# Scan of a bidirectional RWKV-7 block: the next unit's six operand loads are issued by ScalarE at the end of its slot instead of by SyncE

## What is computed

```
state = state * w_t + (state @ -kk_t) (kk_t * a_t)^T + v_t k_t^T      # 64 x 64 per head
y_t   = state @ r_t
```

## Time and profile before

| | us |
|---|---|
| median of 3 runs | 3510.02 (3507.2 to 3510.7) |
| the profiled execution | 3510.56 |
| its span, first to last instruction | 3508.8 |
| TensorE busy | 3421.2 (98%) |
| GpSimd busy | 1681.6 (48%) |
| VectorE busy | 1507.3 (43%) |
| ScalarE busy | 1109.3 (32%) |

### The profile page before, as it was taken

One profiled execution on the slowest core, in us unless ns is written; L12 is line 12 of the kernel. 1 busy time (PEld: TensorE's weight loads), 2 busy tenths in 40 slices (PEclk: granted clock), 3 DMA queues, 4 the chain that ended last, 5 costly groups with the idle time before them and its releaser, 6 DMA issues.

```text
span 3508.8 us, 42655 instructions
## 1 busy us (share of the span) xinstructions
PE 3421.2 (98%) x16463; PEld 2785.3 (79%) x16463; DVE 1507.3 (43%) x1844; ACT 1109.3 (32%) x1756; POOL 1681.6 (48%) x1413
## 2 busy tenths in 40 slices
PE   7999999999998999999799999999999999999999
PEld 6777777777777988888578888888888888888887
DVE  3555445555667877874342023321331133213320
ACT  4333324444234554544342232211221122212221
POOL 4333333333338888887275434444443444444443
PEclk9999999999999999999899999999999999999999
DMA  4444444333355555553543323323333233333323
GB/s 153 120 126 126 123 120 150 115 111 91 105 146 122 127 130 143 123 135 92 201 144 120 120 84 96 96 91 102 96 96 102 90 96 97 99 102 96 96 90 114
DMA packets 663161, 402.25 MB, mean 115 GB/s; under 512 B 191374, under 2 KB 595018, under 8 KB 662506
## 3 DMA queue, kind: packets, MB, share of 16 engines
q1 hardware_dynamic: 663018, 400.34, 39.6%
HBM read 345.73 MB, written 54.53 MB: 114 GB/s over the span
## 4 chain that ended last, share of the span: by engine, by line
PE 50%; DVE 1%; ACT 0%; DMA 0%; POOL 0%; issue 0%; SPq 0%; DVEq 0%; ACTq 0%; POOLq 0%
PE f_bank L149 9%; PE f_bank L151 9%; PE f_bank L150 9%; PE f_bank L1952 5%; PE f_bank L1951 5%; PE f_bank L1953 5%; PE f_bank L1910 2%; PE f_bank L1912 2%; PE f_bank L1911 2%; PE f_bank L1855 1%; PE f_bank L1856 1%; PE f_bank L1857 1%; DMA act_plain<-yt 0%; PE f_bank L1888 0%; POOL w_lo_b L140 0%; PE f_bank L1864 0%
## 5 line engine op out<-in xcount | busy, mean ns | idle before, releaser
L140 POOL TENSOR_TENSOR w_lo_b<-w_raw_b,w_hi_b 128x2048 fp32r<-128x2048 f32 (+1 forms) x152 | 682.0, 4487 | 929.3 <-ACT w_hi_b L133 929.3
L1249 POOL TENSOR_TENSOR ring_w_rounded<-ring_w_plain,ring_w_hi 128x1024 fp32r<-128x1024 f32 x138 | 332.3, 2408 | 617.9 <-ACT ring_w_hi L1262 617.9
L149 PE MATMUL f_bank<-act_rounded,w_lo_b 128*128 128x512 f32 x1408 | 549.1, 390 | 2.4 <-POOL w_lo_b L140 1.2
L133 ACT CAST w_hi_b<-w_raw_b 128x2048 fp32r<-128x2048 f32 (+1 forms) x152 | 283.1, 1862 | 838.3 <-PE f_bank L1953 376.1
L151 PE MATMUL f_bank<-act_rounded,w_hi_b 128*128 128x512 f32 x1408 | 547.8, 389 | 0.0
L150 PE MATMUL f_bank<-act_rounded,w_hi_b 128*128 128x512 f32 x1408 | 547.8, 389 | 0.0
L1519 PE MATMUL slab_ps<-h_hi,ring_w_rounded 128*128 128x512 f32 x1088 | 450.2, 414 | 2.8 <-DVE h_lo L1374 2.5
L1520 PE MATMUL slab_ps<-h_lo,ring_w_hi 128*128 128x512 f32 x1088 | 425.3, 391 | 0.0
L1521 PE MATMUL slab_ps<-h_hi,ring_w_hi 128*128 128x512 f32 x1088 | 425.2, 391 | 0.0
L149 PEld LDWEIGHTS f_bank<-act_rounded,w_lo_b 128*128 128x128 f32 x1408 | 264.3, 188 | 57.5 <-issue 2.2
L151 PEld LDWEIGHTS f_bank<-act_rounded,w_hi_b 128*128 128x128 f32 x1408 | 264.3, 188 | 54.9
(11 more groups left out here) (342 smaller groups left out, 5593.5 us busy)
## 6 DMA issues: line engine op xcount, KB each, us to landing
ring_w_plain<-in_w_in_dram SPq DMA_DIRECT2D x190, 512.0 KB, 4.1
w_raw_b<-in_w_ffn_gate_dram SPq DMA_DIRECT2D x44, 1024.0 KB, 5.2
w_raw_b<-in_w_ffn_up_dram SPq DMA_DIRECT2D x44, 1024.0 KB, 5.2
w_raw_b<-in_w_ffn_down_dram SPq DMA_DIRECT2D x32, 1024.0 KB, 5.0
zt<-slab_out SPq DMA_DIRECT2D x65, 256.0 KB, 4.4
w_raw_b<-in_w_out_dram SPq DMA_DIRECT2D x16, 1024.0 KB, 5.0
w_raw_b<-in_w_ffn_down_dram SPq DMA_DIRECT2D x16, 768.0 KB, 4.4
zt<-lout SPq DMA_DIRECT2D x40, 256.0 KB, 4.6
```

The lines of the kernel that those rows point to most:

```text
L133: act.copy(g.w_hi[n.slot][:, 0:k, :], g.w_raw[n.slot][:, 0:k, :]).then_inc(g.w_hi_ready, 1)
L140: pool.tensor_tensor(g.w_lo[n.slot][:, 0:k, :], g.w_raw[n.slot][:, 0:k, :], g.w_hi[n.slot][:, 0:k, :].bitcast(F32), ALU.subtract).then_inc ...
L149: pe.matmul(bank, wl, hi[:, ka, :], start=start and j == 0, stop=False)
L1249: pool.tensor_tensor(raw_half(w_lo, h), raw_half(w_raw, h), hi_half(h).bitcast(F32), ALU.subtract).then_inc(lo_ready, 1)
```

## The change

The function `load` moves out of SyncE's program, takes the issuing engine as an argument, and is called by ScalarE at the end of each of its slots, behind the copy of half a gate slab. The two waits move with it. The very first load, `load(0)`, stays with SyncE.

```
+        def load(eng, n):
+            s, h, at = place(n)
+            rows = lambda base: zt[base + h * (NQ * P):base + (h + 1) * (NQ * P), at:at + CH].rearrange("(q p) c -> p q c", p=P)
+            for dst, base in ((sw_in, ROW_SW + s * RW), (kk_in, ROW_KK), (ic_in, ROW_IC + s * RW), (k_in, ROW_RKV + RW),
+                              (r_in, ROW_RKV), (v_in, ROW_RKV + 2 * RW)):
+                eng.dma_start(dst[:, :, :], rows(base)).then_inc(landed, 16)
...
             @block.sync
             def _(sp):
-                def load(n):
...
-                load(0)
+                load(sp, 0)
...
                     for h in next_halves(slot + 1)[1:]:
                         weights(h)
-                    if 0 <= w < NUNIT - 1:
-                        sp.wait_ge(taken_dve, DVE_AT["operands", w])
-                        sp.wait_ge(taken_act, ACT_AT["vbd", w])
-                        load(w + 1)
                     if 0 <= u < NUNIT:
...
                     for h in next_halves(slot + 1)[:1]:
                         high(h)
+                    w = unit_at(slot, "w")
+                    if 0 <= w < NUNIT - 1:
+                        act.wait_ge(taken_dve, DVE_AT["operands", w])
+                        act.wait_ge(taken_act, ACT_AT["vbd", w])
+                        load(act, w + 1)
```

## The result

The changed kernel takes 3527.32 us, the median of 5 runs (3522.24 to 3535.42), beside 3510.56 for the kernel before on the same chip. One of the five runs of the kernel before took 5190.07 us, and the ratio goes by the others. It is 1.0046, with a 95% interval of 1.0031 to 1.0061. The forecast was 3504.0, the range 3499 to 3520: wrong in sign, and outside the range. The profiled execution has 3527.32 us as well, 16.8 more than the one of before.

What follows compares the result with a forecast made beforehand. TensorE and GpSimd were taken to bound the scan side by side. At most 7.2 us gained, less 1.6 where TensorE is slower again, plus 0.5 at the start, gave 6.1: profiled 3504.5, median 3504.0, range 3499 to 3520.

Steps and rivals of the forecast that it cites:

- What it adds: ScalarE's six issues delay x1's copy and lx: 0.43 us lost into an odd slot, about 0.1 into an even one.
- The second term mis-sized: Length of the six-load group on ScalarE at SyncE's price, 0.507 us the usual issue: 3.12 us usually, 3.55 on average.
- the 0.5 us: Ahead of GpSimd's iteration 0: the `nb` store lands sooner without 512 KB before it, 0.5 us gained once (0 to 1.5).
- What was removed: In odd slots the loads go out earlier, 7.4 us in slot 21, so TensorE's 11.7 us of waits at yh go.
- 38.3 us a pair: TensorE's pair of slots without 14.6 us of waits: 38.3 us instead of 39.4, less than GpSimd's 38.65.
- The cap of 7.2 us: Gain bounded by GpSimd's idle time, 8.0 us in 7 waits, less 0.12 us for each handover that stays.
- GpSimd: GpSimd's chain in the scan: 38.65 us an iteration, assumed not to depend on what runs beside it.
- The check values: Signs of being right: small waits at `cum`, L811 and GpSimd, issues of 3.1 to 3.6 us, x1 of unit 30 earlier.
- The sign named for a wrong prediction: TensorE waits before lx (L768) for ScalarE's x1 more than 8 us, which was next to nothing before.
- rival 1: Two issuers obstruct each other in odd slots, groups up to 6.2 us: 10 us slower, 3520; chance 0.11.
- (2): An issue costs ScalarE more than SyncE, 0.8 us each, group 4.8: 16 us slower, 3526; chance 0.07.
- (3): Waits at yh go and as much appears before lx through the delayed x1: 3510, within 2; chance 0.15.

Runs made afterwards that it cites:

- hold of six copies: The kernel before, no DMA moved, but ScalarE waits for the operands and makes six unused chained copies, 2.6 us: 3507.65 us, ratio 0.9995.
- kernel 3: The changed kernel, but ScalarE issues the six loads only at the end of odd slots, SyncE in even ones: 3517.30 us, ratio 1.0012.
- hold of nine copies: The kernel before, no DMA moved, but ScalarE waits for the operands and makes nine unused chained copies, 3.9 us: 3521.04 us, ratio 1.0043.
- 5: The changed kernel, but SyncE sends the first half slab behind the `nb` store, not at the slot's start: 3512.38 us, ratio 1.0008.
- kernel 9: The changed kernel, but SyncE waits for ScalarE's copy of x1 before it issues the half slab: 3514.71 us, ratio 1.0007.
- 3.0 (hold): The kernel before, no DMA moved, but ScalarE waits for the operands and makes seven unused chained copies, 3.0 us: 3514.43 us, ratio 1.0000.
- kernel 11: The changed kernel, but ScalarE issues in even slots only and the first half slab goes behind the `nb` store: 3507.71 us, ratio 0.9989.
- kernel 7: The kernel before, all loads on SyncE, but the half slab goes out ahead of the six loads: 3510.50 us, ratio 1.0003.

## Why the prediction was wrong, point by point

**The step that failed** is the overlap claimed in this sentence of "What it adds": "*Into an even slot* `a_bd` is earlier: lx starts 4.3 to 6.8 us behind it", and the loss of "about 0.1" an even slot that came from it. The trace gives 23.5 us of waits at lx into the 13 even slots 2 to 26, 1.8 each. Into the 14 odd slots it gives 6.0 us, 0.43 each, which is what was forecast; the last 1.2 us stand at units 28, 29 and 31 and were there before.

Three things make up the 23.5 us. As an estimate, take the distances from `a_bd` to lx of the kernel before and put the group and the copies behind `a_bd`. With groups of 3.55 us the 13 slots lose about 4 us, 0.3 each, because a gate copy stands ahead of x1's in five of them and not in slot 18 alone. With the groups as measured, 4.28 us on average here, they lose about 10. The other 13 us can come only from cover that has shrunk: x1's weight loads began 2.2 us behind `a_bd` on average over these slots, and begin 1.0 behind it now (slot 7: 2.9 and 0.4). The prediction took this distance for fixed.

Why it shrank is not shown. One reading is that the cover was made of TensorE's own stalls, which the change was to remove: at yh TensorE was kept back, so x1 came late. For it: the distance stays at 2.2 with the hold of six copies, where the waits at yh stay. Against it: in kernel 3 these waits are gone and the distance is still 2.0. The other is that VectorE's operands come later because lx does (below). In the hold of nine copies, where only ScalarE's lateness was added, it is 1.55.

**The second term mis-sized** is the group: 3.55 us by the earlier trace rows, 3.92 measured. The price of one issue was right within 5%. What was left out is what the freed SyncE sends next: the prediction saw that the half slab moves away from the `nb` store, counted 0.5 us for it at the start of the chain, and didn't ask what it moves next to. The `nb` store did land sooner (SyncE's waits for it fall from 51.7 to 29.8 us), but iteration 0 starts at 1030.23, before 1030.03, so the 0.5 us didn't come. Kernels 5 and 9 show that this half is worth most of the loss: with the slab elsewhere the group is 3.4 or 3.3 us and the ratio 1.0008 or 1.0007. Ordered by how long ScalarE is kept behind the operands, all kernels that keep it at this place tell the same:

| ScalarE kept, us | waits at lx, us | ratio |
|---|---|---|
| 2.6 (hold) | 3.0 | 0.9995 |
| 3.0 (hold) | 7.7 | 1.0000 |
| 3.28 (9) | 10.0 | 1.0007 |
| 3.39 (5) | 13.8 | 1.0008 |
| 3.9 (hold) | 23.8 | 1.0043 |
| 3.92 (changed) | 30.7 | 1.0046 |

Up to 3 us no cost can be seen (upper end of the interval 1.0010, 3.5 us), and between 3.4 and 3.9 the time rises by 0.35% by the ratios, by 0.25% by the medians. The likely reason for the steepness is a closed loop: a late copy of x1 makes lx late, lx makes VectorE's xadd wait (44.8 us against 23.9), with it the next operands, and with those the next group of loads. From x1's weight loads to the end of the operands slots 1 to 26 take 19.5 us on average, before 18.3. No kernel cut that loop open, so this part is argued.

**What was removed**: right as a mechanism, worth nothing that can be measured here. The loads are early and the waits at yh go; but in the kernels with less of the stretch (3, 5, 9) the time comes back before the bonus sum (14.4 us to 20.2, 20.5 and 19.2) and at lx. The prediction took TensorE without its own waits, 38.3 us a pair, to be limited by GpSimd alone. By where these waits are, VectorE's chain was the next bound, and the view from which the earlier trace rows came had the row, its largest, 14.4 us in 10 times: the bonus sum's waits for `b_in`. The prediction used it as cover for x1's copy and not as a bound. No kernel made that chain shorter, so that it is the bound is read and not tried. The cap of 7.2 us was no forecast of the gain but an upper bound read as one.

**GpSimd**: an iteration takes 38.4 us, before 38.65, so the assumption that it doesn't depend on what runs beside it held within 1%. Its last operation ends at 1672.28, 15.8 us later: 19.8 us more of waits for `blocks` (27.8 against 8.0), less about 4 that 16 quicker iterations save.

**The check values**: `cum`'s waits below 3 us: 9.0. L811 below 2: 2.1. GpSimd below 2.5: 27.8. Group 3.1 to 3.6: 3.92. x1 of unit 30 at 1656 to 1658: 1679.3. The sign named for a wrong prediction, over 8 us of waits at lx, came with 30.7. Read as the prediction reads it, that would have been rival 1 or 2, and it was neither.

**The rivals**: (1), two issuers in each other's way, falls with kernel 3; in 9, too, 57 of ScalarE's issues overlap one of SyncE's and are short. (2) had nearly the time, 3526, for a wrong reason: an issue costs 0.53 us, not 0.8. (3), the delayed x1 gives back what the odd slots win, is the right kind, but it was priced as a draw: 29.5 us more at lx stand against 9.6 less at yh. None had the slab.

**The accounts**: TensorE's waits from 985 on (without the phase change) rise from 53.3 to 65.4 us, 12.1 of the 16.3. The rest, 4.2 us, lies within what the clock can account for, at most 5 us (last section). That was not tried by itself, and falls of the clock are not what sets this kernel apart: kernel 9's profiled execution has four in the same stretch.

**Left open**: why the cover in even slots shrank; why it is the fifth load that becomes long, and what fills when a 512 KB transfer has just been issued; a smaller slab wasn't tried. Whether kernel 11 is really faster than before by more than a few us would take many more runs.

## What to carry to other kernels

An issue moved onto an engine that computes is paid by the first instruction behind it: price the whole group as a hold of that in-order engine, and ask in the same breath what the freed queue will send earlier, and beside what. Cover that is measured in the kernel before need not be there in the kernel after: here it fell from 2.2 to 1.0 us between the operands and x1. Leave a margin for that. A cheap stand-in, the kernel before with the engine held for so many microseconds, tells how much hold is free, here 3 us; two of them, of 3.0 and of 3.9 us, would have bracketed the sign. It doesn't tell how long the group will be.

## What the hardware showed that was not expected

**The issue time of a load depends on what was issued just before it on another queue.** In the changed kernel 19 groups follow a half slab by 0.1 to 1.5 us. They take 3.33 to 5.31 us, most of the excess in the fifth load (2.27 us in slot 7), but for one of 3.15 in slot 19. The eight that follow one by 1.5 us or more, with none inside them, take 3.15 to 3.31, but for one of 3.57 in slot -1. The same on one queue: 3.78 us on average in kernel 7. A half slab isn't the only cause: in kernel 9 the group of slot 4 takes 3.93 us with the last half slab 10.5 us ahead. Overlap of two issuers with small loads costs nothing (42 issues in kernel 3, none over 0.535 us).

**The granted clock falls behind a short stall of TensorE.** The windows view of the changed kernel around the stall of slot 7, in steps of 3 us (length, busy of five engines, PEclk, DMA share, GB/s):

```profile
1240.00:1243.00 3.00, 1.21 (x8) 0.73 (x6) 1.43 (x3) 0.00 (x0) 2.69 (x5) 1.00 1.19 309
1243.00:1246.00 3.00, 2.06 (x9) 2.06 (x10) 0.00 (x0) 0.58 (x1) 2.68 (x5) 0.57 1.21 325
1246.00:1249.00 3.00, 3.00 (x23) 2.87 (x21) 2.27 (x5) 0.02 (x1) 2.61 (x5) 0.86 0.58 207
1249.00:1252.00 3.00, 3.00 (x23) 2.76 (x22) 2.93 (x5) 2.88 (x8) 2.76 (x4) 1.00 0.00 0
```

TensorE is busy 1.21 of 3 us, and then the granted clock is 0.57 and 0.86 for the next two windows, 1.2 GHz for most of the first, before it is back at 2.4. Between units 2 and 28 the changed kernel has this three times (1243, 1387, 1447), behind stalls of the weight loads of 2.6 to 3.3 us; the kernel before has it not once there. A stall then costs more than its own length: (1 - 0.57) x 3 + (1 - 0.86) x 3 = 1.7 us at most in this case, and as much for each of the other two by the same reckoning, 5 us at most for the three.
